# A forget gate as native float32 products on four column groups, with three reordered steps around it

## The reference, cut to what is touched

```python
def even_mixer(h, w_in, b_f, g_v, w_s, b_s, g_qn, g_kn, w_out):      # h = rms_norm(x, g_mix)
    z = h @ w_in                                      # 1024 -> 2568 columns
    ...                                               # u, v (512 each), q, k, vv (512 each)
    f_logit = z[..., o + 3 * FOX_WIDTH:] + b_f        # the last 8 columns: the forget gate
    log_f = jax.nn.log_sigmoid(f_logit)
    q = rms_norm(q, g_qn)                             # per head of 64
    k = rms_norm(k, g_kn)
    y_a = chunk_gmlp(u, v, g_v, w_s, b_s)             # u * (W_s v + b), W_s is 128 x 128 per group
    y_b = forgetting_attention(q, k, vv, log_f)       # logits + cumulated log_f
    return jnp.concatenate([y_a, y_b], axis=-1) @ w_out
```

## Time and profile before

| | |
|---|---|
| median of 3 runs | 1921.65 us (1921.65 to 1921.85) |
| the profiled execution | 1922.33 us |
| its span, first to last instruction | 1920.5 us |
| PE busy | 1890.9 us, 98% of the span |
| granted TensorE clock, mean | 0.998 |

### The profile page before, as it was taken

The page is one execution under the profiler, slowest core; times in us unless marked ns, Lnnn a source line. Parts: engine busy times, 40 slices in busy tenths (PEclk is TensorE's granted clock), DMA queues, the critical chain, the costliest instruction groups (busy, mean ns, idle before and its releaser), DMA issues.

```text
span 1920.5 us, 22808 instructions
## 1 busy us (share of the span) xinstructions
PE 1890.9 (98%) x8677; PEld 1548.9 (81%) x8677; DVE 948.9 (49%) x1241; ACT 686.2 (36%) x1011; POOL 911.5 (47%) x409
## 2 busy tenths in 40 slices
PE   7999999999999999999999999999999999999999
PEld 6777888888888878788788888888788878888887
DVE  6877945444421248654555444213855474445201
ACT  4556333232323344443632232222234543222211
POOL 2564645444444444644545444445445444445442
PEclk9999999999999999999999999999999999999999
DMA  5242122322323323123232332333233223232322
GB/s 177 68 126 66 67 66 88 109 87 92 102 80 102 117 67 99 34 75 123 67 110 87 100 97 89 97 99 104 80 129 110 82 74 108 88 109 87 99 87 78
DMA packets 165175, 178.91 MB, mean 93 GB/s; under 512 B 4696, under 2 KB 152656, under 8 KB 164849
## 3 DMA queue, kind: packets, MB, share of 16 engines
q1 hardware_dynamic: 162092, 172.10, 28.1%
q10 hardware_dynamic: 3013, 5.84, 1.0%
HBM read 175.83 MB, written 2.10 MB: 93 GB/s over the span
## 4 chain that ended last, share of the span: by engine, by line
PE 61%; issue 21%; POOL 12%; DVE 3%; ACT 2%; DMA 0%; POOLq 0%; ACTq 0%; DVEq 0%
PE acc L529 19%; PE acc L531 18%; PE acc L530 18%; POOL w_lo L2317 10%; PE aux L606 1%; PE aux L737 1%; PE acc L737 1%; POOL prob_e L2412 1%; PE aux L529 0%; PE aux L531 0%; PE aux L530 0%; PE acc L903 0%; DVE a_lo L1172 0%; PE aux L663 0%; POOL xp L2401 0%
## 5 line engine op out<-in xcount | busy, mean ns | idle before, releaser
L2317 POOL TENSOR_TENSOR w_lo<-w_raw,w_hi 128x1024 fp32r<-128x1024 f32 x322 | 793.0, 2484 | 867.7 <-ACT w_hi L1860 867.7
L529 PE MATMUL acc<-a_hi,w_hi 128*128 128x512 f32 (+1 forms) x1480 | 582.9, 394 | 2.1 <-DVE a_lo L1172 1.4
L531 PE MATMUL acc<-a_hi,w_lo 128*128 128x512 f32 (+1 forms) x1480 | 577.8, 390 | 0.0
L530 PE MATMUL acc<-a_lo,w_hi 128*128 128x512 f32 (+1 forms) x1480 | 577.5, 390 | 0.0
L1860 ACT ACTIVATE w_hi<-w_raw 128x1024 fp32r<-128x1024 f32 x324 | 325.0, 1051 | 445.7 <-PE acc L531 418.0
L529 PEld LDWEIGHTS acc<-a_hi,w_hi 128*128 128x128 f32 (+1 forms) x1480 | 277.9, 188 | 71.7 <-issue 8.1
L531 PEld LDWEIGHTS acc<-a_hi,w_lo 128*128 128x128 f32 (+1 forms) x1480 | 277.9, 188 | 59.5
L530 PEld LDWEIGHTS acc<-a_lo,w_hi 128*128 128x128 f32 (+1 forms) x1480 | 278.1, 188 | 58.7 <-issue 1.2
L529 PE MATMUL acc<-h_hi,w_hi 128*128 128x512 f32 x528 | 205.8, 390 | 0.0
L531 PE MATMUL acc<-h_hi,w_lo 128*128 128x512 f32 x528 | 205.4, 389 | 0.0
L530 PE MATMUL acc<-h_lo,w_hi 128*128 128x512 f32 x528 | 205.4, 389 | 0.0
(11 more groups left out here) (407 smaller groups left out, 2256.4 us busy)
## 6 DMA issues: line engine op xcount, KB each, us to landing
w_raw<-in_w_gate SPq DMA_DIRECT2D x22, 1024.0 KB, 5.2
w_raw<-in_w_up SPq DMA_DIRECT2D x22, 1024.0 KB, 5.2
w_raw<-in_w_down SPq DMA_DIRECT2D x16, 896.0 KB, 4.9
w_raw<-in_hy_w_in SPq DMA_DIRECT2D x12, 1024.0 KB, 5.7
w_raw<-in_ffn_w_gate SPq DMA_DIRECT2D x11, 1024.0 KB, 5.2
w_raw<-in_ffn_w_up SPq DMA_DIRECT2D x11, 1024.0 KB, 5.2
w_raw<-in_e_w_in SPq DMA_DIRECT2D x10, 1024.0 KB, 5.1
w_raw<-in_xa_wkv SPq DMA_DIRECT2D x8, 1024.0 KB, 5.0
```

The source lines that it names most:

```text
L529: nc.tensor.matmul(o, l_hi, r_hi, start=start, stop=False)
L530: nc.tensor.matmul(o, l_hi, r_lo, start=False, stop=False)
L531: return nc.tensor.matmul(o, l_lo, r_hi, start=False, stop=stop)
L2317: nc.gpsimd.tensor_tensor(w_lo[s][:, half], w_raw[s][:, half], w_hi[s][:, half].bitcast(F32), ALU.subtract)\
```

## The change

- `forget_gate`: the narrow f block is gone (its load on SP, its split on ACT, its remainder on POOL, its 24 products). In its place stand 8 native float32 products between the two u blocks, of the unrounded x with the gate's weights `w_gate` (128 x 8 x 8, loaded by one DMA from ACT's queue at the end of the SwiGLU before, and multiplied by the norms' gains by one DVE instruction). Products of channel tiles g and 4+g write rows 32g to 32g+7 of one `aux` bank, so that four column groups of the array are used.
- DVE adds up the four partial rows (one copy, three additions, 8x512 each) ahead of `rstd`, and later scales the sum by `rstd`.
- `gmlps` goes from inside the first q block to between the two q blocks.
- The transposes of q go from between the two k blocks into the second k block, ahead of its last token tile.
- On DVE the norms of k come ahead of the low parts of q; on ACT the first two squares of k come ahead of the high parts of q, and the split before them is done earlier.

```diff
@@ PE
+        def forget_gate():
+            operand()
+            bank = open_aux("gate")
+            for first in (0, 4):
+                for g in range(4):
+                    last = nc.tensor.matmul(bank[32 * g:32 * g + HEADS, :], w_gate[:, first + g, :], x[:, first + g, :],
+                                            start=first == 0, stop=first == 4)
+            last.then_inc(aux_ready, 1)
+
         wide_block(a_hi, a_lo, inside=even_sums, wait_from=0)
+        forget_gate()
         wide_block(a_hi, a_lo, between=even_roots)
...
         token_blocks(a_hi, a_lo, TT, name="g")
-        wh, wl = block_in(KT, 8, whole=True)
-        bank = open_acc("f")
-        open_acc("f spare")
-        for k in range(KT):
-            last = exact(bank[0:8, :], wh[:, k, :], wl[:, k, :], a_hi[:, k, :], a_lo[:, k, :], k == 0, k == KT - 1)
-        last.then_inc(acc_ready, 2)
-        block_done(2)
-        token_blocks(a_hi, a_lo, TT, name="q", inside=gmlps)
+        token_blocks(a_hi, a_lo, TT, name="q", between=gmlps)
...
-        token_blocks(a_hi, a_lo, TT, name="k", between=lambda: head_transposes("q", q_raw))
+        token_blocks(a_hi, a_lo, TT, name="k", inside=lambda: head_transposes("q", q_raw), inside_at=(1, 3))
@@ DVE
+        dve.wait_ge(in_gate, 16)
+        for_pe(V.tensor_tensor(w_gate, w_gate, small[:, 80:80 + KT].rearrange("p (k one) -> p k one", one=1)
+                               .to_broadcast([P, KT, HEADS]), ALU.mult))
         free_aux(V.tensor_copy(sums, take_aux()[:, 0:8]), again=True)
...
+        partial = take_aux()
+        step(V.tensor_copy(gate[:, :], partial[0:HEADS, :]))
+        for r in (32, 64, 96):
+            (free_aux if r == 96 else step)(V.tensor_tensor(gate[:, :], partial[r:r + HEADS, :], gate[:, :], ALU.add))
         free_aux(V.tensor_copy(rstd[:, :], take_aux()), again=True)
...
-        ins = V.tensor_tensor(gate[:, :], f_bank[0:8, :], rstd[0:8, :], ALU.mult)
...
+        step(V.tensor_tensor(gate[:, :], gate[:, :], rstd[0:8, :], ALU.mult))
...
-        heads_low(q_hi, q_lo, small[:, 1:2])
         normalized_heads(k_raw, 0, 2)
+        acted(PAIRS)
         normalized_heads(k_raw, 2, 4)
+        heads_low(q_hi, q_lo, small[:, 1:2], rounded=True)
         heads_low(k_hi, k_lo, par("e_g_kn_2"))
@@ ACT
+        act.dma_start(w_gate, ins["e_w_in_2"][0].rearrange("(k p) c -> p k c", p=P)[:, :, 2560:2560 + HEADS]).then_inc(in_gate, 16)
...
-        split_next()
         given()
-        evac.next(2)
         step(S.activation(tmp[4][0:8, :], gate[:, :], ACT.Abs))
...
         spatial_high(3)
+        split_next()
+        raw_squares("k", k_raw, 0, 2)
         heads_high("q", q_hi, small[:, 1:2])
-        split_next()
-        raw_squares("k", k_raw, 0, 4)
+        raw_squares("k", k_raw, 2, 4)
@@ SP
         token(w, 512)
-        wide(w, 2560, 8)
```

More of the change, by code:

```diff
@@ L329, in build @@
     row_small = put("row_small", [P, P])
+    w_gate = row_small[:, 64:128].rearrange("p (k h) -> p k h", k=KT)
     masks = at("masks", [P, 3 * P], F32R, offset=sq_at)
@@ L429, in build @@
     in_half = [sem(f"in_half{h}") for h in range(2)]
-    in_even, in_pool = sem("in_even"), sem("in_pool")
+    in_even, in_pool, in_gate = sem("in_even"), sem("in_pool"), sem("in_gate")
     in_x_again = sem("in_x_again")
@@ L439, in build @@
     INVERSE_TABLE = 13
-    FOX_BLOCK = 18 + FT + 12 + 11 + 2
+    FOX_BLOCK = 18 + FT + 12 + 10 + 2
     CROSS_BLOCKS = [FOX_BLOCK + 2, FOX_BLOCK + 2 + 8 + FT + 12 + 8 + 4]
@@ L560, in wide_block, with token_blocks @@
             block_done(outs)
-        def token_blocks(l_hi, l_lo, tiles, name=None, between=None, inside=None):
+        def token_blocks(l_hi, l_lo, tiles, name=None, between=None, inside=None, inside_at=(0, 2)):
             banks = []
@@ L567, in token_blocks @@
                 for t in range(tiles):
-                    if inside and (b, t) == (0, 2):
+                    if inside and (b, t) == inside_at:
                         inside()
@@ L1508, in _ @@
         dve.wait_ge(acc_free, acc_read.value())
-        take_acc()
-        f_bank = acc[:, (n_acc[0] - 1) % 4, :]
-        take_acc()
-        ins = V.tensor_tensor(gate[:, :], f_bank[0:8, :], rstd[0:8, :], ALU.mult)
[L1513 to L1516, removed]
+        step(V.tensor_tensor(gate[:, :], gate[:, :], rstd[0:8, :], ALU.mult))
         for_act(V.tensor_scalar(gate[:, :], gate[:, :], small[0:8, 0:1], None, ALU.add))
@@ L1565, in normalized_heads, with heads_low @@
             (signal_with if end == TT else lambda ins, _: step(ins))(ins, scaled)
-        def heads_low(hi, lo, gain):
+        def heads_low(hi, lo, gain, rounded=False):
             for i in range(PAIRS):
                 bank = take_aux()
-                acted()
+                if not rounded:
+                    acted()
                 free_aux(V.scalar_tensor_tensor(lo[:, i, :], bank, gain, hi[:, i, :].bitcast(F32), ALU.mult, ALU.subtract))
```

## The result

| | before | after |
|---|---|---|
| median of 20 runs | 1921.08 us (1920.01 to 1921.85) | 1924.14 us (1920.02 to 1925.45) |
| ratio | | 1.0014, 95% interval 1.0008 to 1.0020 |
| profiled execution, span | 1922.33, 1920.5 us | 1922.44, 1920.5 us |
| granted clock, mean over a run | 0.998 | 0.996 or 0.997 in 17 of the 20 runs, 0.999 in three (1920.0 to 1920.5 us) |

The change makes the kernel 3 us slower by the medians where 3.5 us less were forecast, though the program has 55 instructions fewer. That is still within 0.2% of before, but above the range given (1917.5 to 1920.4).

The account below looks back on a forecast made before the run. PE was taken to bound the kernel, busy 1890.9 of 1920.5 us. Old gate -5.53, new gate +1.97, spatial products +0.10 gave -3.46 us: 1918.2 from the median 1921.65, range 1917.5 to 1920.4.

Parts of the forecast that it names:

- The gate: New gate on PE, four column groups at once: 1.72 + 0.16 + 0.09 = 1.97 us, replacing the old gate's 5.53.
- Rivals 1 to 3: New gate's column groups: two at a time, gain 1.75 (0.09); strict order, gain 1.3 (0.05); not parallel, 1.5 us slower (0.04).
- The spatial products: Behind the first q block PE waits 0.16 us for scaled g instead of 0.06, a loss of 0.10 us.
- q: q's transposes moved 8.2 us later: q scaled 0.7 to 1 us after the first k block, so no wait.
- k: At k's transposes: k scaled 5 to 6 us after k's blocks end, needed 10.9 after; no wait priced.
- Rival 4: A wait at k's banks, or DVE late for the spatial products under POOL's halves, takes 1 to 2.4 us; chance 0.07.
- The clock: First q block to end of v: PE taken at the full clock, 2.4 GHz; no term for a lower one.
- What would show it wrong: Prediction wrong if starts pair or come singly, PE waits at a moved step, or shifts at v's end and span's end differ.
- Rival 5: Every later block changes its slot; later stalls depending on that give perhaps 0.5 us more gain, 1917.7; chance 0.05.

Follow-up runs that it names:

- x2: Kernel before plus the new gate and the moved spatial products; q's transposes and the order of k's norms as before; 1927.25 us, ratio 1.0033.
- x4: Changed kernel, POOL making the weight remainder of the four k and v blocks for only 32 columns of each half, rest stale; 1917.82 us, ratio 0.9984.
- x7: Kernel before with seven useless buffer clearings on DVE ahead of k's last scaling; 1928.57 us, ratio 1.0042, four runs.
- x1: Kernel before plus the new gate alone; spatial products, q's and k's steps as before; 1925.98 us, ratio 1.0028.

## Why the prediction was wrong

- **The gate: right.** 1.97 us forecast, 2.02 measured; four groups run four at a time. Rivals 1 to 3 fell. By an estimate from the figures of the Trainium skill ("TensorE: Matmul & The Clock Gate", Part 3, measured speedup) it would have been some 0.5 us dearer, which the trace doesn't show.
- **The spatial products: right.** A wait of 0.16 us was forecast, 0.15 came.
- **q: right in what came of it, wrong in the count.** There is no wait at its transposes. But q was forecast scaled 0.7 to 1 us after the end of the first k block, and it was scaled at 750.01, 6.1 us after that end (36 products ahead of 752.08, so 743.9). The 8.2 us by which the transposes were moved covered an error of 5 us; with them in their old place PE waits 6.0 us (x2). That was luck.
- **k: wrong, and this is the step that failed.** "DVE is done with k at 5 to 6 us after the end of k's blocks" took the old distance from that end, less 3.1 us of low parts and one hit of POOL. It tied DVE's chain to the end of k's blocks, but in the kernel after the chain doesn't wait for them: it starts with the spatial products and runs through. Between these and the end of k's blocks PE now has half a q block less, 24 products or 5.4 us. Measured from that end (756.56), DVE was done with k after 13.2 us and not after 5 to 6. PE asked after 11.2, so DVE was 2.0 late, with the freed bank 2.8. The paragraph on q named the true anchor ("these start as late after g as before"), but neither count used it. The hits of POOL, 12.9 us instead of 11.0 over the chain, took another 1.9 where I had counted on one fewer. Only where POOL's halves are taken away does the forecast hold: in x4 k is scaled 5.5 us after the end of k's blocks.
- **Rival 4 was the right mechanism**, with 0.07. It had the place, k's banks, but its size, 1 to 2.4 us, was too small: 2.96 us are lost ahead of the transposes and 1.54 more in them. Here -3.46 forecast, with +0.05 at the gate, -0.01 at the spatial products and +4.50 at k, makes +1.08; the distance grew by 1.39. Of the last 0.3 us 0.23 are a wait of PE for POOL's second half for v's first block: the products at 757.69, 758.05 and 758.38 are 0.36 and 0.33 us apart instead of 0.23 (POOL's halves for it run from 753.23 to 757.99).
- **The clock was counted as full.** The rest of the 3.1 us by the medians goes with it. The equal spans of the two profiled executions are chance. The one of after comes to `even_sums` 1.64 us later, behind stretches at a lower granted clock from 24 to 32 us (0.78 and 0.79) and from 176 to 180 (0.57) where before has 1.00; it comes to the attention 3.03 later; at the products of the earlier trace rows it is 1.4 later, and at the end 0, because before has such stretches near 905 (0.64) and 1497 (0.62) and after has none there. So the end of v was 1.4 us later, counted from `even_sums`, and the end of the span not at all. Of the 20 runs of after 17 have a mean of 0.997 or lower, and the three at 0.999 took what before took. x7 shows that a wait of PE brings the lower level behind it; where it lay in the runs without a profile isn't known, and so the split of the 3.1 us into a wait and a clock is not shown run by run.
- **What would show it wrong** was named: a wait of PE, and a shift at the end of v that isn't that at the end. The trace has both; the wait is at k's transposes, whose own place the change had left alone while it moved the work around them. Rival 5, more than the sum, was not seen: the most that any distance fell is 3.36 (x4).

## What to carry to other kernels

When a step is moved on the bounding engine, measure the path of each helper engine from the step that starts its chain to the step that needs its end, and compare that with the bounding engine's work between the same two steps. The end of some block is no anchor if the helper doesn't wait for it. Here DVE was busy for 85% of that path and had 0.4 us to spare at its end, so there was no room for a path 5.2 us shorter, and behind a gap of 3.0 to 5.5 us (after, x7, x1) PE lost another 1.5 to 2.7 at the lower clock or for banks. The shorter PE work was worth something only once the splits on ACT, and with them POOL's work, had been placed anew.

## What the hardware showed that was not expected

- Four column groups (8 columns each, 512 streamed) ran four at a time: 16 instructions with starts over 1.3 us, 592 ns each, as one alone. With the way in and out they cost 2.02 us, 0.30 more than four steps of 0.43.
- Shortening POOL's work in four blocks shortened DVE's chain by 7.7 us (51.25 to 43.58) and its busy time by 12.7, though DVE's own instructions were the same. Small instructions pay most for their size: a 128x16 one goes from 0.17 to 2.3 us. q's low parts, 128x512 with one input in PSUM, paid nothing (3.11 us for four, with and without POOL).
- 2 us or more of waiting on PE were followed by the lower clock in all nine profiled executions that had them in this stretch, and waits of 1.3 us or less in none of three.
